# Layer-norm scales and offsets from 16-partition rows spread by matmuls, in place of 1 MB broadcast loads

## The chip, the cores and the metric

The kernel runs on one core of one Trainium2 chip. The metric is device microseconds of that core for one execution, and the median over the runs that were timed. TensorE is written PE, VectorE DVE, ScalarE ACT, GpSimd POOL, SyncE SP. SP issues nearly all plain loads; POOL issues the gathers; all of them are carried by the same 16 DMA engines.

## The reference

For 256 tokens of width 1024 (two blocks of 128 tokens, `tb` 0 and 1), in float32:

```python
for i in range(2):                                   # layers
    mix = mlstm_mixer(x, ...) if i == 0 else mla_mixer(x, ...)
    x = layer_norm(ALPHA * x + mix, ln_g[i, 0], ln_b[i, 0])
    x = layer_norm(ALPHA * x + peer_ffn(x, ...), ln_g[i, 1], ln_b[i, 1])
    x = x + sigmoid(x @ ple_w_gate[i]) * (p[i] @ ple_w_proj[i])
# then second_block: a hybrid attention mixer, a SwiGLU, and a last RMS norm with norm_final_g

def layer_norm(x, g, b):
    y = (x - mean(x)) * rsqrt(var(x) + eps)
    return y * g + b                                 # g, b: 1024 values, the same for all tokens

def peer_ffn(x, w_q, sub_keys, u, v):                # per token: 8 heads, top 16 experts of 16384 each
    act = gelu(u[experts] . x)                       # 128 rows of u a token
    return sum(gates * act * v[experts])             # 128 rows of v a token
```

Every token needs 128 rows of 8 KB (the row of `u` and the row of `v` side by side in `in_uv`) in each of the two layers.

## The kernel before

Tokens lie on the 128 partitions, features along them. The expert rows are the bulk of the traffic: there are four windows `r` = 0 to 3 (layer `r // 2`, token block `r % 2`), and each gathers 128 rows a token as 128 indirect DMAs of 1 MB (128 partitions x 8 KB), L1196, two to a group `k`, 64 groups a window. Eight slots of `gath` hold them. The ring of one group is: POOL waits for `row_free` and issues two gathers; DVE takes the dot product of each landed row with `xt` (L1845); ACT applies Gelu; DVE multiplies with the gate (L1856); ACT scales the `v` half (1024 wide, line 1211); PE adds it, turned, into two held PSUM banks (16 matmuls, L546) and increments `row_free`.

All other work of a window is cut into slots, and `weave` runs so many slots in each group, on each engine between its `head(k)` and its `tail(k)`. The order is the same list of names on PE, ACT and DVE: `sum`, `ple`, `mla`, `attend`, `out`, `pq` (queries and scores of the next layer's experts, the choice of experts on DVE). So the rest of the work moves at the pace of the gathers. Window 0 runs `first_slots`, windows 1 and 2 `next_slots(0)` and `next_slots(1)`, window 3 `last_slots`. What follows the last gather has no gathers beside it.

Weights go through a ring of four slots of 2 MB. `take` on PE appends a load to `loads`, and SP issues the list in order, each as soon as the slot's last use is over. `aux` appends a load of another kind to the same list: the two arrays of a layer norm come this way. `in_lnp` holds them already copied for each of the 128 partitions, so that one `aux` brings `lnp` (128 partitions x 2 x 1024 values). There are six: the first ahead of window 0, then one in `first_slots` (slot 12), one in each `mla_slots` (slot "cq a") and one in each `pq_slots` (slot 6). `ln_apply` on DVE waits for `sem("lnp")`, multiplies by `lnp[:, 0, :]` (L1606) and adds `lnp[:, 1, :]` (L1607). Where the next block of tokens uses the same arrays, `fresh=False`.

PSUM banks are handed out in turn by `open_` (a held bank is passed over), `close` says that a bank is full, and `evac` on ACT copies it out and frees it; `moved` waits for that.

A plain float32 matmul of the code is two MATMUL instructions in the trace (a transpose is one).

Of the kernel before, what the change touches and what calls it, by code (L numbers as in the profile page):

```python
# [14 lines left out]
P = 128  # L15
# [3 lines left out]
KC = D // P  # L19
# [44 lines left out]
X_LAYER = 3  # L64
# [54 lines left out]
def program(nc, a, out, ctx, dbg):  # L119
    def sb(name, shape, dt=F32):  # L120
        return ctx.enter_context(nc.sbuf_tensor(name, shape, dt))
# [13 lines left out]
    yt = sb("y_tok", [P, TB, D])  # L135
    xT = sb("xT", [P, KC, T])
    lnp = sb("lnp", [P, 2, D])
    ident = sb("ident", [P, P])
    identa = sb("identa", [P, P])
    ones = sb("ones", [P, P])  # L140
# [27 lines left out]
    slot_loaded = [sem(f"slot_loaded{i}") for i in range(NW)]  # L168
    x_ready = [sem(f"x_ready{tb}") for tb in range(TB)]
    xn_ready = [sem(f"xn_ready{tb}") for tb in range(TB)]  # L170
    place = {}
    uses = [0] * 8

# [121 lines left out]
    def _(pe):  # L295
# [54 lines left out]

        def aux(dst, src, key, after=None):
            loads.append(dict(kind="aux", dst=dst, src=src, sem=sem(key), after=after))

        def rows(w, c0, n):
            return w[:, c0:c0 + n].rearrange("(k p) n -> p k n", p=P)
# [244 lines left out]
        def mla_slots(tb):  # L600
            transposes("xM", xt, KC, tb, x_ready[tb], X_PLE)
            yield "turn x"
            yield "move x"
            await_T("xM", tb)
            w, rec = take(rows(a["kv_w_down_r"], 0, 512), KC, 512)
            tok(f"ckv_{tb}", xT, w, cols(tb), KV_RANK, KC, slice(0, KV_RANK))
            yield "ckv"
            wq, rq = take(rows(a["b_w_dq"][0], 0, Q_RANK), KC, Q_RANK)
            aux(lnp[:, :, :], a["lnp"][1, 0], "lnp", (x_ready[tb], X_PEER))
            tok(f"cq_{tb}", xT, wq, cols(tb), Q_RANK, KC, ks=range(0, 4))  # L610
            yield "cq a"
            tok(f"cq_{tb}", xT, wq, cols(tb), Q_RANK, KC, ks=range(4, 8))
            last_use(rq, f"cq_{tb}")
            yield "cq b"
            o = open_(f"kr_{tb}")
            for e in range(2):
                ins = feat(o, e * P, w, xT, slice(KV_RANK + e * P, KV_RANK + (e + 1) * P), range(KC), KC, cols(tb))
            close(ins, f"kr_{tb}")
            last_use(rec, f"kr_{tb}")
            yield "kr"  # L620
            yield "rms"
            yield "rms sqrt"
            yield "rms scale"
            pe.wait_ge(sem("c_ready"), tb + 1)
            for nm, c0, n in ((f"ckvT_{tb}", 0, 2), (f"cqT_{tb}", KV_RANK, 3)):
                o = open_(nm)
                for k in range(n):
                    ins = nc.tensor.transpose(o[:, k * P:(k + 1) * P], yt[:, tb, c0 + k * P:c0 + (k + 1) * P],
                                              ident[:, :])
                close(ins, nm)  # L630
            yield "turn c"
            yield "move c"
            moved(pe, f"ckvT_{tb}")
            moved(pe, f"cqT_{tb}")
            wu, rec = take(rows(a["kv_w_up"], 0, 2048), 2, 2048)
            for half in range(2):
                nm = f"kn_{tb}_{half}"
                o = open_(nm)
                for j in range(4):
                    h = half * 4 + j  # L640
                    ins = feat(o, j * P, wu, M["ckvT"], slice(h * 256, h * 256 + 128), range(2), 2, slice(0, P))
                close(ins, nm)
            yield "kn"
            wv = ring[:, rec["slot"], 0:4096].rearrange("p (k h e n) -> p k h e n", k=2, h=H, e=2)
            for half in range(2):
                nm = f"kvv_{tb}_{half}"
                o = open_(nm)
                for k in range(2):
                    ins = mm(o[:, :], M["ckvT"][:, k, :], wv[:, k, half * 4:half * 4 + 4, 1, :], k == 0, k == 1)
                close(ins, nm)  # L650
            last_use(rec, f"kvv_{tb}_1")
            yield "kvv"
            for half in range(2):
                w, rec = take(rows(a["b_w_uq_p"], half * 768, 768), 3, 768)
                nm = f"qn_{tb}_{half}"
                o = open_(nm)
                for j in range(4):
                    ins = feat(o, j * P, w, M["cqT"], slice(j * P, (j + 1) * P), range(3), 3, slice(0, P))
                close(ins, nm)
                nm = f"qr_{tb}_{half}"  # L660
                o = open_(nm)
                for e in range(2):
                    ins = feat(o, e * P, w, M["cqT"], slice((4 + e) * P, (5 + e) * P), range(3), 3, slice(0, P))
                close(ins, nm)
                last_use(rec, nm)
                yield f"q {half}"
            yield "move q"
            yield "rope"
# [66 lines left out]
        def pq_slots(l, tb):  # L735
            transposes(f"xT{l + 1}", xt, KC, tb, x_ready[tb], l * X_LAYER + X_MIX)
            yield "turn x"
            yield "move x"
            await_T(f"xT{l + 1}", tb)
            for i in range(PQ_SLOTS):  # L740
                if i < 8:
                    pq_half(l, tb, i // 2, i % 2)
                if i % 2 == 1 and 0 <= (i - 3) // 2 < 4:
                    scores(l, tb, (i - 3) // 2)
                if i == 6:
                    aux(lnp[:, :, :], a["lnp"][1 if tb else 0, 1], "lnp", (x_ready[tb], X_LAYER + X_MIX))
                yield f"pq {i}"

        def first_slots():
            for i in range(FIRST_SLOTS):  # L750
                if i < 4:
                    pq_half(0, 0, 2 + i // 2, i % 2)
                if i in (1, 3, 5):
                    scores(0, 0, 1 + i // 2)
                if i == 4:
                    transposes("xT1", xt, KC, 1, x_ready[1], X_MIX)
                if i == 6:
                    await_T("xT1", 1)
                if 6 <= i < 14:
                    pq_half(0, 1, (i - 6) // 2, i % 2)  # L760
                if i == 12:
                    aux(lnp[:, :, :], a["lnp"][0, 1], "lnp", (x_ready[1], X_MIX))
                for j, at in enumerate((9, 11, 15, 20)):
                    if i == at:
                        scores(0, 1, j)
                yield f"first {i}"
# [351 lines left out]
    def _(pool):  # L1118
# [19 lines left out]
                          allow_small_or_imprecise_dtypes=True))  # L1138
        step.wait()
        pool.tensor_scalar(identa[:, :], ident[:, :], ALPHA, None, ALU.mult).then_inc(sem("consts"), 1)  # L1140
        pool.wait_ge(sem("gates"), 1)
        for dst, src in ((xt[:, :, :], a["x"].rearrange("(b p) d -> p b d", p=P)), (A["g"][:, :], a["hng"]),
                         (posi, a["pos"]), (invf[:, :], a["invf"])):
# [62 lines left out]
    def _(act):  # L1206
# [21 lines left out]
        def evac_T(name, dst, tb):  # L1228
            for g in range(2):
                evac(f"{name}_{tb}_{g}", dst[:, 4 * g:4 * g + 4, cols(tb)], split(4))  # L1230


        act.wait_ge(sem("c_loaded"), 16)
# [92 lines left out]
        def mla_slots(tb):  # L1326
# [10 lines left out]
            yield "kr"  # L1337
            evac(f"kr_{tb}", M["tk"], split(2))
            yield "rms"
            sqrt(2)  # L1340
            yield "rms sqrt"
            yield "rms scale"
            yield "turn c"
            evac(f"ckvT_{tb}", M["ckvT"], split(2))
# [42 lines left out]
        def pq_slots(l, tb):  # L1387
            n0 = UNIT_BASE[l * TB + tb]
            yield "turn x"
            evac_T(f"xT{l + 1}", xT, tb)  # L1390
            yield "move x"
            for i in range(PQ_SLOTS):
                if i % 2 == 0 and 0 <= (i - 2) // 2 < 4:
                    queries(l, tb, (i - 2) // 2)
                if i % 2 == 0 and 0 <= (i - 4) // 2 < 4:
                    scores(l, tb, (i - 4) // 2)
                m = (i - CHOOSE_FROM - USTEPS) // USTEPS
                if (i - CHOOSE_FROM) % USTEPS == 0 and 0 <= m < UNITS:
                    gate_exp(n0 + m)
                yield f"pq {i}"  # L1400

        def first_slots():
            for i in range(FIRST_SLOTS):
# [5 lines left out]
                    sqrt(1)  # L1409
                if i == 5:  # L1410
                    evac_T("xT1", xT, 1)
                if i in (8, 10, 12, 14):
                    queries(0, 1, (i - 8) // 2)
                for j, at in enumerate((10, 12, 16, 21)):
# [159 lines left out]
    def _(dve):  # L1574
# [2 lines left out]
        nsq = [0]  # L1577
        nln = [0]

        def inverse_sd(n):  # L1580
            nsq[0] += 1
            dve.wait_ge(sem("sd_ready"), nsq[0])
            step(v.reciprocal(rstd[:, 0:n], sdv[:, 0:n]))
# [8 lines left out]
        def ln_apply(tb, src, frees=(), fresh=True, y=None):  # L1592
# [8 lines left out]
                else:  # L1601
                    step(ins)
            if fresh:
                nln[0] += 1
                dve.wait_ge(sem("lnp"), 16 * nln[0])
            step(v.tensor_tensor(y, y, lnp[:, 0, :], ALU.mult))  # L1606
            v.tensor_tensor(xt[:, tb, :], y, lnp[:, 1, :], ALU.add).then_inc(x_ready[tb], 1)  # L1607

# [647 lines left out]
        for tb in range(TB):  # L2256
# [1 line left out]
            dve.wait_ge(x_ready[tb], X_HYBRID + 1)  # L2258
            sum_squares(tb)
            inverse_sd(1)  # L2260
            dve.wait_ge(sem("lnp"), 16 * (nln[0] + 1))
            v.scalar_tensor_tensor(yt[:, tb, :], xt[:, tb, :], rstd[:, 0:1], lnp[:, 0, :], ALU.mult, ALU.mult
                                   ).then_inc(sem("out_ready"), 1)

# [56 lines left out]
```

## Time and profile before

| | |
|---|---|
| median of 3 runs | 2259.17 us (2254.94 to 2259.38) |
| profiled execution: its own time | 2258.05 us |
| its span, first to last instruction | 2256.3 us |
| busy: PE, DVE, ACT, POOL | 1715.9, 1216.9, 907.2, 595.8 us |
| moved by DMA | 777.21 MB, mean 344 GB/s |
| chain that ended last | PE 43%, DMA 31%, DVE 15%, ACT 5%, POOL 3% |

The busy times are sums over the span, and the engines overlap. The chain is followed back from the last instruction, at each step to what released it. The table averages over three parts with different limits: a start of 200 us, the gathers, and an end of some 476 us.

### The profile page before, as it was taken

Reading aid. Unit: us, or ns where it says so; the run is one execution under the profiler, and the core shown is the slowest. Engines: PE = TensorE matmul, PEld = TensorE weight load, DVE = VectorE, ACT = ScalarE, POOL = GpSimd, SP = SyncE. Lnnn points to the kernel's source line nnn. Section 1 sums busy time; section 2 is a strip of 40 time slices with the busy share of each in tenths; the row PEclk is TensorE's granted clock in tenths of the full one; section 3 lists DMA queues with packets and bytes.
Section 4 is the critical chain, followed back from the end, with each engine's and each line's share of the span. In section 5 each row is a group of like instructions: output and inputs, shape, how many; then the busy total and the mean of one; then the engine's idle time right before and its main releaser. Section 6 shows DMA issues by size and latency. Waiting matters only on the chain.

```text
span 2256.3 us, 25092 instructions
## 1 busy us (share of the span) xinstructions
PE 1715.9 (76%) x9720; PEld 1405.1 (62%) x9720; DVE 1216.9 (54%) x3105; ACT 907.2 (40%) x1294; POOL 595.8 (26%) x569
## 2 busy tenths in 40 slices
PE   8998755555767786576778656778877779989998
PEld 6458644445556675455657645468777468868863
DVE  3647687886544559854555896455534255610001
ACT  1113454455544544554455445455654212510000
POOL 1002233444333332333333335543323000000000
PEclk9999876777888797689879867878998888999999
DMA  7639999999999999999999999999999768664350
GB/s 268 244 103 376 415 400 411 400 408 421 386 418 413 416 415 408 405 394 417 413 415 415 397 413 411 409 400 413 410 411 414 274 224 299 235 224 149 112 191 33
DMA packets 183335, 777.21 MB, mean 344 GB/s; under 512 B 11584, under 2 KB 19328, under 8 KB 115888
## 3 DMA queue, kind: packets, MB, share of 16 engines
q0 software_dynamic: 74720, 539.80, 58.4%
q1 hardware_dynamic: 107920, 235.15, 28.3%
q8 instruction: 77, 1.26, 0.2%
q10 hardware_dynamic: 576, 0.66, 0.1%
q14 instruction: 42, 0.34, 0.0%
HBM read 774.52 MB, written 1.05 MB: 344 GB/s over the span
## 4 chain that ended last, share of the span: by engine, by line
PE 43%; DMA 31%; DVE 15%; ACT 5%; POOL 3%; issue 3%; another core or an unknown queue 0%; SPq 0%; DVEq 0%; POOLq 0%; ACTq 0%
PE bank L318 34%; DMA arena<-in_uv,eidx 25%; PE bank L546 9%; DVE arena L1845 5%; DMA ring<-in_peer_w_q 3%; ACT arena L1211 3%; DMA ring<-in_w_in_2r 3%; POOL arena L1196 3%; DVE y_tok L1776 2%; DVE y_tok L1772 1%; ACT L1211 1%; DVE y_tok L1812 1%; DVE y_tok L1813 1%; DVE y_tok L1809 1%; DVE mid_region L1768 0%
## 5 line engine op out<-in xcount | busy, mean ns | idle before, releaser
L546 PE MATMUL bank<-ident,arena 128*128 128x128 f32 x4096 | 663.9, 329 | 421.5 <-ACT arena L1211 421.1
L546 PEld LDWEIGHTS bank<-ident,arena 128*128 128x128 f32 x4096 | 586.3, 171 | 499.4 <-ACT arena L1211 487.9
L1845 DVE CUSTOM_DVE_ANT_0 arena<-arena,x_tok 128x1024 f32<-128x1024 f32 x512 | 621.4, 1224 | 493.7 <-DMA arena<-in_uv,eidx 493.3
L1196 POOL DMA_INDIRECT arena<-in_uv,eidx x512 | 576.3, 1126 | 1139.8 <-PE bank L546 900.8
L1211 ACT ACTIVATE arena<-arena,coef 128x1024 f32<-128x1024 f32 x512 | 559.9, 1141 | 285.2 <-DVE coef L1856 277.0
L318 PE MATMUL bank<-xT,ring 128*128 128x128 f32 (+2 forms) x3104 | 478.0, 317 | 64.7 <-DMA ring<-in_w_in_2r 24.6
L318 PEld LDWEIGHTS bank<-xT,ring 128*128 128x128 f32 (+1 forms) x3104 | 441.5, 202 | 100.2 <-DMA ring<-in_w_in_2r 26.4
L1211 ACT ACTIVATE glu<-dots 128x2 f32<-128x2 f32 x256 | 52.0, 203 | 438.0 <-DVE dots L1845 432.4
L318 PE MATMUL bank<-ring,xT 128*128 128x512 f32 (+3 forms) x384 | 164.2, 583 | 0.0
L1211 ACT ACTIVATE arena<-bank 128x256 f32<-128x256 f32 (+1 forms) x62 | 30.0, 490 | 301.1 <-PE bank L318 295.9
L1211 ACT ACT_TABLE_LOAD x112 | 143.7, 1283 | 2.8 <-PEq L2313 0.8
L318 PEld LDWEIGHTS bank<-ring,xT 128*128 128x128 f32 x384 | 77.2, 207 | 72.1 <-issue 66.0
L318 PE MATMUL bank<-ring,arena 128*128 128x512 f32 x272 | 117.8, 593 | 2.4 <-ACT arena L1211 1.0
L318 PEld LDWEIGHTS bank<-ring,arena 128*128 128x128 f32 x272 | 51.4, 190 | 65.8 <-issue 64.7
L2253 DVE TENSOR_TENSOR arena<-arena,bank 128x256 f32<-128x256 f32 x22 | 9.3, 421 | 150.3 <-PE bank L318 150.3
L1211 ACT ACTIVATE mid_region<-bank 128x512 f32<-128x512 f32 (+7 forms) x108 | 50.4, 493 | 86.8 <-PE bank L318 86.7
L1856 DVE TENSOR_TENSOR coef<-glu,gate 128x2 f32<-128x2 f32 x256 | 41.1, 160 | 64.1 <-ACT glu L1211 60.8
L318 PE MATMUL bank<-ring,mid_region 128*128 128x128 f32 (+1 forms) x240 | 70.3, 440 | 0.5 <-ACT mid_region L1211 0.5
L1625 DVE SCALAR_TENSOR_TENSOR ring<-ring,silu_cT 128x512 f32<-128x512 f32 x84 | 63.2, 752 | 3.0
L318 PE MATMUL bank<-mid_region,ring 128*128 128x128 f32 (+1 forms) x400 | 52.1, 292 | 7.3 <-ACT mid_region L1211 7.3
L318 PEld LDWEIGHTS bank<-mid_region,ring 128*128 128x128 f32 x400 | 51.2, 211 | 7.9 <-ACT mid_region L1211 7.8
L1211 ACT ACTIVATE sdv<-var 128x1 f32<-128x1 f32 (+2 forms) x17 | 3.5, 204 | 129.3 <-DVE var L2048 100.5
(243 smaller groups left out, 1134.0 us busy)
## 6 DMA issues: line engine op xcount, KB each, us to landing
ring<-in_w_in_2r SPq DMA_DIRECT2D x20, 2048.0 KB
ring<-in_peer_w_q SPq DMA_DIRECT2D x16, 2048.0 KB
ring<-in_w_ada SPq DMA_DIRECT2D x12, 2048.0 KB
ring<-in_ple_w_gate SPq DMA_DIRECT2D x8, 2048.0 KB
ring<-in_a_w_in SPq DMA_DIRECT2D x6, 2048.0 KB
ring<-in_w_ffn_gate SPq DMA_DIRECT2D x5, 2048.0 KB
ring<-in_w_ffn_up SPq DMA_DIRECT2D x5, 2048.0 KB
ring<-in_w_ffn_down SPq DMA_DIRECT2D x5, 2048.0 KB
```

The lines of the kernel that those rows point to most:

```text
L318: return nc.tensor.matmul(o, l, r, start=start, stop=stop)
L546: ins = nc.tensor.matmul(bank(f"pe{l}_{tb}_{c // 4}")[:, (c % 4) * P:(c % 4 + 1) * P], gath[:, s, D + c * P:D + (c + 1) * P], ident[:, :], ...
L1196: pool.indirect_dma_start(gath[:, i % SLOTS, :], None, a["uv"], bass.IndirectOffsetOnAxis(ap=eidx[:, tb, i:i + 1], axis=0)).then_inc(sem(f ...
L1211: return nc.scalar.activation(o, i, fn, **kw)
L1625: ins = v.scalar_tensor_tensor(w[:, k, :], w[:, k, :], scT[:, k:k + 1], w[:, k - 1, :], ALU.mult, ALU.add)
L1772: step.go(v.max(vals[:, i, lo:lo + 8], s[:, i, :]))
L1776: step.go(v.max_index(idx[:, i, lo:lo + 8], vals[:, i, lo:lo + 8], s[:, i, :]))
L1809: step(v.tensor_tensor(eq, p12f[:, e, :, :].unsqueeze(3).broadcast_to([P, UH, 16, 16]), iota16[:, :].unsqueeze(1).unsqueeze(1).broadcast_t ...
L1812: step(v.tensor_tensor(eq, eq, i4[:, :, e, :].unsqueeze(2).broadcast_to([P, UH, 16, 16]), ALU.mult))
L1813: step(v.tensor_reduce(i12[:, e, :, :], eq, AX, ALU.add))
L1845: v.tensor_tensor_reduce(out=gath[:, s, 0:D], in0=gath[:, s, 0:D], in1=xt[:, tb, :], scale=1.0, scalar=0.0, op0=ALU.mult, op1=ALU.add, acc ...
L1856: v.tensor_tensor(coef[:, s:s + GRP], glu[:, s:s + GRP], gate[:, tb, k * GRP:(k + 1) * GRP], ALU.mult).then_inc(sem("coef"), 1)
```

## The change

The five norms after the first take their two arrays from `ln_rows`, a small tile. At the start POOL loads, for each of the three pairs (layer, norm) that occur, the 2 x 1024 values once, as 16 rows of 128 values on 16 partitions (partitions 0, 32 and 64 onwards); 8 KB each. Before a norm, `spread(i, e)` on PE (array e of norm i; ten calls) writes the array to all 128 partitions of two PSUM banks: eight matmuls, each with one column of the identity, broadcast to 16 x 128, as the weights and the 16 rows as the moving operand. ACT copies the two banks into `lnp` one slot later, after a wait that the last reader of `lnp` is done. DVE waits for four banks to be moved where it waited for one DMA. Five of the six `aux` loads of `in_lnp` go.

```diff
+        def spread(i, e):                       # PE
+            at = SPREAD_AT[SPREAD[i]]
+            if i == 0 and e == 0:
+                pe.wait_ge(sem("ln_rows"), 16 * len(SPREAD_AT))
+            for half in range(2):
+                nm = f"ln{i}_{e}_{half}"
+                o = open_(nm)
+                for c in range(4):
+                    row = e * KC + half * 4 + c
+                    ins = mm(o[:, c * P:(c + 1) * P], ident[at:at + 16, at + row:at + row + 1].broadcast_to([16, P]),
+                             ln_rows[at:at + 16, :])
+                close(ins, nm)
...
             wq, rq = take(rows(a["b_w_dq"][0], 0, Q_RANK), KC, Q_RANK)
-            aux(lnp[:, :, :], a["lnp"][1, 0], "lnp", (x_ready[tb], X_PEER))
...
             yield "kr"
+            spread(1 + 2 * tb, 0)
             yield "rms"
+            spread(1 + 2 * tb, 1)
             yield "rms sqrt"
...
-                if i == 6:
-                    aux(lnp[:, :, :], a["lnp"][1 if tb else 0, 1], "lnp", (x_ready[tb], X_LAYER + X_MIX))
+                if i in (11, 12):
+                    spread(2 + 2 * tb, i - 11)
...
-                if i == 12:
-                    aux(lnp[:, :, :], a["lnp"][0, 1], "lnp", (x_ready[1], X_MIX))
+                if i in (22, 23):
+                    spread(0, i - 22)
...
+        for (l, i), at in SPREAD_AT.items():    # POOL, behind the constants, ahead of its wait for "gates"
+            pool.dma_start(ln_rows[at:at + 16, :], a["lnp"][l, i, 0].rearrange("e (c n) -> (e c) n", n=P)
+                           ).then_inc(sem("ln_rows"), 16)
...
+        def spread(i, e):                       # ACT
+            for half in range(2):
+                evac(f"ln{i}_{e}_{half}", lnp[:, e, half * 512:half * 512 + 512], whole)
...
             yield "rms"
+            act.wait_ge(x_ready[tb], X_PEER)
+            spread(1 + 2 * tb, 0)
             sqrt(2)
             yield "rms sqrt"
+            spread(1 + 2 * tb, 1)
...
+                if i in (12, 13):
+                    act.wait_ge(x_ready[tb], X_LAYER + X_MIX)
+                    spread(2 + 2 * tb, i - 12)
...
+                if i in (23, 24):
+                    act.wait_ge(x_ready[1], X_MIX)
+                    spread(0, i - 23)
...
+        def norm_loaded():                      # DVE, in ln_apply
+            if nln[0] == 0:
+                dve.wait_ge(sem("lnp"), 16)
+            else:
+                for e in range(2):
+                    for half in range(2):
+                        moved(dve, f"ln{nln[0] - 1}_{e}_{half}")
+            nln[0] += 1
```

## Rows read from the trace of the kernel before

**Rows 1.** The page's 40 slices: busy tenths by engine, then DMA share and GB/s.
```profile
DVE  3647687886544559854555896455534255610001
...
DMA  7639999999999999999999999999999768664350
GB/s 268 244 103 376 415 400 411 400 408 421 386 418 413 416 415 408 405 394 417 413 415 415 397 413 411 409 400 413 410 411 414 274 224 299 235 224 149 112 191 33
```

**Rows 2.** Stretches: from:to, length, busy us (instructions) by engine, PEclk, DMA share, GB/s.
```profile
200.00:1780.00 1580.00, 1092.33 (x6802) 951.61 (x6800) 976.35 (x2498) 795.79 (x1081) 578.50 (x536) 0.81 1.00 406
1780.00:2256.30 476.30, 441.94 (x2157) 336.31 (x2156) 135.19 (x273) 78.06 (x156) 0.55 (x1) 0.94 0.52 187
```

**Rows 3.** DMA queues of the page: packets, MB, share of 16 engines over the span.
```profile
q0 software_dynamic: 74720, 539.80, 58.4%
q1 hardware_dynamic: 107920, 235.15, 28.3%
```

**Rows 4.** Waits over the span: engine line <- releaser: total us, times, longest us.
```profile
POOL arena L1196 <- PE bank L546: 900.8, 222, 21.3
DVE arena L1845 <- DMA arena<-in_uv,eidx: 493.3, 317, 9.5
...
POOL x_tok L1144 <- DVE mid_region L1667: 16.1, 1, 16.1
```

**Rows 5.** DMA issues: the loads into lnp, count and size of each.
```profile
lnp<-in_lnp SPq DMA_DIRECT2D x6, 1024.0 KB
```

**Rows 6.** Timeline of SyncE's queue: start us, us taken, instruction, count.
```profile
221.33 22.27 SPq L1111 DMA_DIRECT2D lnp<-in_lnp  x1
...
598.61 0.66 SPq L1111 DMA_DIRECT2D lnp<-in_lnp  x1
...
823.63 0.58 SPq L1111 DMA_DIRECT2D lnp<-in_lnp  x1
...
998.69 1.22 SPq L1111 DMA_DIRECT2D lnp<-in_lnp  x1
...
1224.36 0.58 SPq L1111 DMA_DIRECT2D lnp<-in_lnp  x1
```

**Rows 7.** Chain of waits, in order: start us, us, what; one gather per load.
```profile
265.40 19.89 DMA arena<-in_uv,eidx
...
606.62 14.46 DMA arena<-in_uv,eidx
...
841.96 18.93 DMA arena<-in_uv,eidx
```

**Rows 8.** Chain of waits, 1195 to 1300 us.
```profile
1223.95 28.80 DMA ring<-in_peer_w_q
...
1252.79 6.44 PE bank L318 x32
...
1280.07 1.14 DVE arena L1845
```

**Rows 9.** Two stretches of DVE choosing experts, columns as in rows 2.
```profile
860.00:920.00 60.00, 33.34 (x186) 29.91 (x184) 57.27 (x186) 29.56 (x37) 20.78 (x20) 0.69 1.01 408
1280.00:1340.00 60.00, 29.62 (x144) 25.64 (x144) 57.51 (x198) 27.14 (x33) 18.50 (x19) 0.66 1.02 413
```

**Rows 10.** VectorE's timeline, 838 to 905 us; in brackets its idle time before.
```profile
860.91 1.23 DVE L1845 CUSTOM_DVE_ANT_0 arena<-arena,x_tok 128x1024 f32<-128x1024 f32 x1 [1.53 <-DMA arena<-in_uv,eidx]
```

**Rows 11.** Stretches of 5 us, columns as in rows 2.
```profile
1265.00:1270.00 5.00, 3.28 (x22) 2.91 (x22) 3.50 (x9) 4.48 (x7) 0.00 (x0) 0.85 0.97 405
1270.00:1275.00 5.00, 3.58 (x24) 3.35 (x23) 4.90 (x24) 3.88 (x6) 3.24 (x3) 0.81 0.69 239
```

**Rows 12.** PE timeline, 860 to 900 us: one score, four matmuls in the code.
```profile
862.69 1.06 PE L318 MATMUL bank<-ring,mid_region 128*128 128x128 f32 x8
```

**Rows 13.** Instruction groups by shape: count, busy us, mean ns, idle before.
```profile
L1211 ACT ACTIVATE y_tok<-bank 128x512 f32<-128x512 f32 x22 | 12.9, 590 | 40.2 <-PE bank L318 36.7 <-PE bank L853 2.9 <-issue 0.5
...
L318 PE MATMUL bank<-mid_region 32*128 32x128 f32 x32 | 5.9, 304 | 0.0
```

**Rows 14.** POOL's timeline, 0 to 60 us.
```profile
24.80 0.56 POOL L1144 DMA_DIRECT2D arena<-in_hng  x1
```

More of the change, by code:

```diff
@@ L137, in program @@
     lnp = sb("lnp", [P, 2, D])
+    ln_rows = sb("ln_rows", [P, P])
     ident = sb("ident", [P, P])
@@ L170, in program @@
     xn_ready = [sem(f"xn_ready{tb}") for tb in range(TB)]
+    SPREAD = ((0, 1), (1, 0), (0, 1), (1, 0), (1, 1))
+    SPREAD_AT = {(0, 1): 0, (1, 0): 32, (1, 1): 64}
     place = {}
@@ L1603, in ln_apply @@
             if fresh:
-                nln[0] += 1
-                dve.wait_ge(sem("lnp"), 16 * nln[0])
+                norm_loaded()
             step(v.tensor_tensor(y, y, lnp[:, 0, :], ALU.mult))
@@ L2260, in _ @@
             inverse_sd(1)
-            dve.wait_ge(sem("lnp"), 16 * (nln[0] + 1))
+            dve.wait_ge(sem("lnp"), 16 * 2)
             v.scalar_tensor_tensor(yt[:, tb, :], xt[:, tb, :], rstd[:, 0:1], lnp[:, 0, :], ALU.mult, ALU.mult
```

## The prediction

> **What bounds the kernel now.** I read the 40 slices first, for where each engine is full. The DMA line is at 9 from the fourth slice to the thirty-first, at some 400 to 420 GB/s in nearly all, and falls off behind it; DVE reaches 9 in two [rows 1]. So I cut the span in parts. From 200 to 1780 us, where the gathers run, the DMA share is 1.00 at 406 GB/s, while PE is busy 1092 of 1580 us, DVE 976 and ACT 796; from 1780 us on the DMA share is 0.52 and PE is busy 442 of 476 us [rows 2]. The reader is to see two limits: bytes in the middle, PE at the end. The change takes no byte and no instruction from the end, so whatever it gives or costs is decided before 1780 us.
>
> The waits agree. DVE waits 317 times, 493.3 us in all, for a gathered row, and POOL 222 times, 900.8 us, for PE to free a slot [rows 4]. Both can be true together because a gather is on its way for long: on the chain of waits, single gathers take 19.89, 14.46 and 18.93 us from the end of their issue to the dot product [rows 7]. The price of one gather alone is far smaller: the gathers' queue held the engines for 58.4% of 2256.3 us, 1317.7 us for 539.8 MB [rows 3], which is 2.56 us for one MB (1.0486 million bytes). Some five to eight gathers' worth of bytes thus stand ahead of each, and it is this queue that sets the pace of the groups, and with it that of all slots woven in.
>
> **What goes.** Six loads of 1024 KB fill `lnp` [rows 5]; five go, issued at 221, 599, 824, 999 and 1224 us [rows 6], all inside the full part. Their rows are 8 KB in one piece on each partition, as the gathered rows are, so I price each at a gather's 2.56 us: 12.8 us for five. The nearest other row is SP's own queue, 28.3% of the span for 235.15 MB [rows 3], 638.5 us, 2.85 us for such a load: 14.2 us, the upper end. Spread over the mean rate of 406 GB/s [rows 2] it is 5.243 / 0.406 = 12.9 us. The lower end is nothing. I take 12.8 us as what leaves the queue.
>
> The Trainium skill (DMA: Bandwidth & Descriptors, Where 436 GB/s comes from) has two ceilings, 435 GB/s where the ports bind and about 358 GB/s where a core's share of the HBM does, and says that the second binds for loads from HBM. By 358 the five loads would be 14.6 us, by 435 12.1 us. This trace holds 406 GB/s over 1580 us of such loads [rows 2], so the 358 does not hold on this core.
>
> **Which of it reaches the end.** Bytes taken away shorten the time only if the DMA engines don't run dry between that load and the next gather somebody waits for; otherwise the pause just becomes longer. I went through the five.
>
> The loads of 599 and 999 us stand in stretches where DVE waits for nearly each row; the gather issued at 606.62 us was waited for [rows 7], and no pause follows before the queue's gain is handed on. Both count in full: 5.12 us. The load of 221 us: the gather ended issuing at 265.40 us took 19.89 us, longer than others, with this load and the next weights ahead of it, and DVE waited [rows 7]. I take 2.3 of 2.56 us.
>
> The load of 824 us: the chain goes over a gather that took 18.93 us [rows 7], but DVE had waited only 1.53 us for it [rows 10], and from there it is nearly full, 57.27 of 60 us [rows 9]. So 1.53 us come at once; what is more only shortens the queue and is worth something when DVE is through. Between 1.53 and 2.56 us I take 1.8.
>
> The load of 1224 us stands behind a weight load on the same queue. The chain goes over that weight load, 28.80 us from 1223.95 us on, then over PE from 1252.79 us on, and DVE is still on it at 1280.07 us [rows 8]. PE's stall held the slots back, and the DMA engines ran nearly dry: share 0.97 and then 0.69 in the 10 us from 1265 us on [rows 11], some 0.05 x 5 + 0.33 x 5 = 1.9 us of pause against the 1.02 of full stretches. Without our load the pause comes to 4.5 us, and nobody gains. Then DVE is full again, 57.51 of 60 us [rows 9]. Bounds nothing and 2.56 us; I take 0.3.
>
> One could hope that the weight load itself lands sooner when the `lnp` load is gone, and with it PE's stall. It is issued first, 0.4 us ahead of ours [rows 6, 8]. The Trainium skill (DMA: Bandwidth & Descriptors, Queues, rings and completion order) says that on each DMA engine one queue's descriptors are taken in ring order; by that the load behind does not slow the one ahead, and this stall stays. If it did slow it, the fifth load would count in full and the sum would be 2.3 us better.
>
> Gain: 5.12 + 2.3 + 1.8 + 0.3 = 9.5 us.
>
> **What comes.** PE: ten calls of eight matmuls, 80 in the code and 160 instructions. The nearest row is a score, 8 instructions in 1.06 us at full clock [rows 12], so 2.1 us a call and 21.2 us in all. The upper bound is the row with few weight rows, 32 x 128: 32 instructions, mean 304 ns each by itself [rows 13], 160 x 0.304 = 48.6 us; its busy time, 5.9 us for 32, gives 29.5 us. The expectation is near the lower value. PE is idle for 488 of the 1580 us [rows 2]. A call delays the rows of its group by 2 to 5 us, and with them the next two gathers; two gathers are 5.1 us of DMA time while 14 to 20 us stand in the queue [rows 7], so the queue doesn't run out. Four of the ten calls come in the choice stretches, where PE is busy 33 and 30 of 60 us [rows 9]. I cost it at nothing. If that cover were gone, it would be the 21 to 49 us themselves.
>
> ACT: twenty copies of a bank, 0.59 us each [rows 13], 11.8 us, in a part where ACT is idle 784 us [rows 2]. In the slot "rms sqrt" two copies come ahead of the square root, 1.2 us later for DVE's normalization, twice; DVE's waits for rows in those stretches cover it. ACT's Gelu is one group ahead of the copies, so DVE's coefficients don't stand behind them. Its new waits on `x_ready` are for steps a dozen slots back. Nothing.
>
> DVE: four bank waits where there was one DMA wait, five norms; all banks were copied many slots before. A passed wait is not in the trace; between nothing and 0.1 us for each of the fifteen more, I take 0.2 us in all. PE's bank rotation moves by two banks a call; the banks come back after six others, long copied. SP loses five issues, one of which held it for 22.27 us [rows 6]; the weights behind it were wanted much later, so nothing. POOL: three more issues, 0.56 us each by a plain one [rows 14], 1.7 us, behind the constants and inside its idle 16.1 us [rows 4]. Their bytes, 24 KB, are 0.06 us.
>
> **Sum.** 9.5 - 0.2 = 9.3 us off the path. The profiled execution took 2258.05 us for a span of 2256.3 us, so 1.75 us lie around it; it would become 2248.75 us. The median of the runs is 1.12 us above this execution; I apply the same difference to it: 2259.17 - 9.3 = 2249.9 us, a change of -0.41%.
>
> **Rivals.** *All five count.* The pause at 1265 us is not independent of our load, the queue hands everything on. Then 12.8 us, 2246.4 us, and with the price of SP's own queue 14.2 us, 2245.0 us. For it: the share is 1.00 over the whole part [rows 2]. Against it: the pause itself [rows 11]. Chance 0.27.
>
> *The queue isn't the limit.* The pace of the groups is that of the loop over PE, ACT and DVE, and faster landing only makes DMA pauses. For it: DVE near full in two stretches [rows 9], POOL's 900.8 us for slots [rows 4]. Against it: 493.3 us of DVE waiting for rows [rows 4]. Only the two loads in stretches without full engines, or less, would count, and the rest of the gain goes: 0 to 4.5 us, 2254.7 to 2259.2 us. Chance 0.14.
>
> *PE's added matmuls decide.* The rows of a group wait for them, the gathers of the next slots are issued later and the queue runs out. If all 21.2 us lay on the path beside the gain of 9.3 us, the time would be 2271.1 us, with 48.6 us 2298.5 us. It is slower than before from the point where 9.3 us of them are on the path, and by over 0.2% from 13.8 us on, 65% of the lower price. For it: PE stands in the ring of each group, and at 1252 us a PE stall did empty the queue [rows 8, 11]. Against it: 488 idle us, and a queue of over 14 us. Chance 0.05.
>
> **How the numbers follow.** The forecast has 0.46: 10.5 us off with the first and third load in full, 8.2 us with 1.53 us for each, and 1.1 us to either side for the step from one execution to the median, so 2247.5 to 2252.5 us. Between it and the second rival, 2252.5 to 2254.7 us, where one more load is lost or some spread calls cost 3 us, lies 0.08. The range from 2244.8 to 2253.8 us takes in the first rival with its dearer price and the forecast, and leaves out the hidden case and the slower one, some 0.2. 0.2% is 4.5 us, about what timing this kernel can tell from no change. Faster by over that: 0.46 + 0.27 + 0.08 = 0.81; within it: 0.14; slower: 0.05.
>
> **What would show it.** The profile after should have five loads fewer, 5.2 MB less, a DMA share still 1.00 and about the same 406 GB/s to the last gather, that gather some 9 us earlier, and the part behind it as long as before (476 us). PE should show 160 instructions more, ACT twenty, and DVE no new wait ahead of L1606. The fifth load's step is right if the pause that follows the last score of window 2 has grown by about 2.5 us, wrong if it hasn't. It would all be wrong if the DMA share fell below 1.00 over the middle with the last gather where it was (the queue was no limit), or if rows came late behind the spread calls.

## The result, and the profile after

The changed kernel has a median of 2247.37 us (2243.91 to 2252.41, 9 runs) beside 2257.91 us for the kernel before (2252.7 to 2262.88, 9 runs): ratio 0.9957, 95% interval 0.9946 to 0.9969, that is 9.7 us less (7.0 to 12.2). The two medians lie 10.5 us apart; the differences in this text go by the ratio, which has the interval. Run again later, it gave 0.9959 (0.9942 to 0.9975), 9.3 us less. The forecast was 9.3 us less.

The page after, first its slices (DVE, DMA share, GB/s), then the DMA queues (packets, MB, share of 16 engines):

```profile
DVE  3648687876544559854455896454534356610001
...
DMA  7639999999999999999999999999999768664350
GB/s 269 246 103 399 415 402 413 403 396 416 401 417 412 417 414 378 400 391 417 413 415 415 391 395 411 410 407 409 413 410 413 279 226 294 248 225 151 113 194 31
```
```profile
q0 software_dynamic: 74816, 539.83, 58.8%
q1 hardware_dynamic: 107200, 229.91, 27.9%
```

SP's queue carries 229.91 MB where it carried 235.15 [rows 3], five loads less; the full part is as full as it was [rows 1]. Cut at its own last gather (from:to, length, busy us with instructions for PE, PEld, DVE, ACT, POOL, then PEclk, DMA share, GB/s):

```profile
200.00:1770.00 1570.00, 1130.34 (x6948) 988.75 (x6949) 975.74 (x2495) 800.86 (x1095) 574.92 (x536) 0.81 1.00 405
1770.00:2242.20 472.20, 436.54 (x2155) 331.85 (x2153) 135.20 (x273) 77.89 (x156) 0.56 (x1) 0.95 0.53 189
```

The gathers' part is 10 us shorter at the same share and rate [rows 2]: fewer bytes, not faster ones. Not all of the 10 us belongs to the change, though. SP issued the weight loads ahead of the first left-out load 4.7 us earlier than before, and the run that keeps all five loads and has the spread calls beside them (below) did it just as early; the profiled execution of the kernel before had lost these microseconds by then. First row before, second after, third the run that keeps the loads:

```profile
201.80 0.99 SPq L1106 DMA_DIRECT2D ring<-in_peer_w_q  x2
197.09 0.99 SPq L1124 DMA_DIRECT2D ring<-in_peer_w_q  x2
197.19 1.00 SPq L1129 DMA_DIRECT2D ring<-in_peer_w_q  x2
```

In the second profile of the changed kernel the last gather was issued at 1746.8 us, against 1742.4 in the first and 1751.6 before. So the size of the effect rests on the runs and their intervals, not on a pair of profiles.

The waits say the same as before [rows 4], with a little less of each:

```profile
POOL arena L1217 <- PE bank L563: 897.0, 227, 17.3
DVE arena L1887 <- DMA arena<-in_uv,eidx: 480.7, 325, 7.0
```

The spreading, as groups by shape (count | busy us, mean ns | idle us before) and two of its ten calls in PE's timeline:

```profile
L322 PE MATMUL bank<-ln_rows,ident 16*128 16x128 f32 x160 | 27.4, 336 | 0.0
L1232 ACT ACTIVATE lnp<-bank 128x512 f32<-128x512 f32 x20 | 10.9, 587 | 7.5 <-PE bank L322 7.5
L1648 DVE TENSOR_TENSOR y_tok<-y_tok,lnp 128x1024 f32<-128x1024 f32 x7 | 8.6, 1225 | 0.2
```
```profile
341.06 3.78 PE L322 MATMUL bank<-ln_rows,ident 16*128 16x128 f32 x16
...
866.77 2.05 PE L322 MATMUL bank<-ln_rows,ident 16*128 16x128 f32 x16
```

The reader is to see three things: 160 instructions as counted, 2.05 us a call at full clock as [rows 12] gave it, and DVE not waiting ahead of its multiplication with `lnp` (0.2 us in seven, and 0.2 us in the kernel before). Four of the ten calls ran at half clock and took 3.78 us, so PE's total is 27.4 us, not 21.2.

This one execution took 2243.91 us, 14.1 us less than the profiled one before, which is more than the 9.7 us of the runs. Some 4 us of the 14.1 arose behind the last gather (472.20 us beside 476.30), in a part that no edit touches; it is told of at the end.

Where the DMA engines paused, and how much, is the part of the prediction that could be wrong. The pause after the scores of window 1, before:

```profile
865.00:870.00 5.00, 4.53 (x40) 4.32 (x40) 4.86 (x14) 4.53 (x8) 1.82 (x2) 1.00 0.98 369
870.00:875.00 5.00, 1.52 (x9) 1.28 (x8) 4.93 (x23) 3.87 (x5) 1.96 (x3) 0.76 0.95 376
```

and after, in window 1 and in window 2:

```profile
850.00:855.00 5.00, 4.86 (x44) 4.66 (x42) 4.41 (x9) 0.70 (x2) 2.92 (x2) 1.00 0.78 283
855.00:860.00 5.00, 3.42 (x20) 3.24 (x21) 3.61 (x8) 4.77 (x6) 0.20 (x1) 0.77 0.82 333
860.00:865.00 5.00, 3.29 (x25) 3.05 (x25) 4.90 (x26) 3.88 (x7) 3.32 (x4) 0.89 0.66 211
```
```profile
1250.00:1255.00 5.00, 4.78 (x43) 4.58 (x41) 4.31 (x9) 0.79 (x2) 2.07 (x2) 1.00 0.98 378
1255.00:1260.00 5.00, 3.50 (x30) 3.32 (x31) 4.09 (x10) 4.77 (x6) 1.09 (x1) 1.00 0.75 306
1260.00:1265.00 5.00, 1.65 (x14) 1.41 (x13) 4.89 (x26) 3.78 (x6) 4.08 (x4) 0.89 0.87 292
```

A pause is counted here as (1.02 - share) x 5 us, summed over the neighbouring rows with a share below 1.00; 1.02 is the share of full stretches. The pause in window 1 was (0.04 + 0.07) x 5 = 0.55 us and is (0.24 + 0.20 + 0.36) x 5 = 4.0 us: it grew by 3.4 us. In window 2 it was 1.9 us [rows 11] and is (0.04 + 0.27 + 0.15) x 5 = 2.3 us. In the second profile of the changed kernel they are 4.0 and 3.4 us.

The weight load ahead of these pauses took as long as before. On the chain of waits it stood with 28.80 us from 1223.95 us on [rows 8]; after, with the `lnp` load behind it gone:

```profile
1214.14 28.64 DMA ring<-in_peer_w_q
```

### The profile page after: what moved, and what is told of

The parts are those of the page before. It is cut to its first block, busy times and chain, and to the rows that moved or that the text cites. A ratio compares the mean times of both kernels' runs of the same rounds, so it can differ in the third digit from the quotient of the medians.

```text
span 2242.2 us, 25444 instructions
## 1 busy us (share of the span) xinstructions
PE 1747.9 (78%) x9880; PEld 1437.5 (64%) x9880; DVE 1217.9 (54%) x3105; ACT 916.7 (41%) x1314; POOL 593.8 (26%) x572
## 3 DMA queue, kind: packets, MB, share of 16 engines
q1 hardware_dynamic: 107200, 229.91, 27.9%
## 4 chain that ended last, share of the span: by engine, by line
PE 46%; DMA 30%; DVE 13%; ACT 6%; POOL 3%; issue 2%; another core or an unknown queue 0%; DVEq 0%; SPq 0%; POOLq 0%; ACTq 0%
PE bank L322 35%; DMA arena<-in_uv,eidx 26%; PE bank L563 10%; DVE arena L1887 4%; ACT arena L1232 3%; DMA ring<-in_peer_w_q 3%; POOL arena L1217 3%; DVE y_tok L1818 1%; ACT L1232 1%; DVE y_tok L1814 1%; DMA ring<-in_w_in_2r 1%; DVE y_tok L1854 1%; DVE y_tok L1855 1%; DVE y_tok L1851 1%; PE bank L399 0%
## 5 line engine op out<-in xcount | busy, mean ns | idle before, releaser
L563 PE MATMUL bank<-ident,arena 128*128 128x128 f32 x4096 | 677.0, 333 | 394.2 <-ACT arena L1232 393.4
L563 PEld LDWEIGHTS bank<-ident,arena 128*128 128x128 f32 x4096 | 598.9, 174 | 471.9 <-ACT arena L1232 459.8
L1887 DVE CUSTOM_DVE_ANT_0 arena<-arena,x_tok 128x1024 f32<-128x1024 f32 x512 | 622.0, 1224 | 481.3 <-DMA arena<-in_uv,eidx 480.7
L322 PE MATMUL bank<-xT,ring 128*128 128x128 f32 (+2 forms) x3104 | 471.4, 314 | 46.5 <-DMA ring<-in_peer_w_q 18.9
L322 PEld LDWEIGHTS bank<-xT,ring 128*128 128x128 f32 (+1 forms) x3104 | 435.5, 199 | 81.1 <-DMA ring<-in_peer_w_q 16.9
```

Source lines behind the costliest of these rows:

```text
L322: return nc.tensor.matmul(o, l, r, start=start, stop=stop)
L563: ins = nc.tensor.matmul(bank(f"pe{l}_{tb}_{c // 4}")[:, (c % 4) * P:(c % 4 + 1) * P], gath[:, s, D + c * P:D + (c + 1) * P], ident[:, :], ...
L1887: v.tensor_tensor_reduce(out=gath[:, s, 0:D], in0=gath[:, s, 0:D], in1=xt[:, tb, :], scale=1.0, scalar=0.0, op0=ALU.mult, op1=ALU.add, acc ...
```

## The experiments

Twelve kernels ran, each beside the kernel before, whose median in these three groups was 2257.0 to 2257.3 us. Ratios are to it. A ratio's interval is some 0.0009 to 0.0015 to either side, 2 to 3.4 us, twice that for the two kernels with four times the spreading, and some 4 us for a difference between two kernels. "The changed kernel" in a difference is its ratio of 0.9957 or 0.9959.

**The parts by themselves.** The changed kernel again:

> The changed kernel once more, beside the three that run with it. Both theories: 9 to 11 us under the kernel before, ratio 0.995 to 0.996 (it measured 0.9957 with an interval of 0.9946 to 0.9969). It is the base for the differences below.

Measured: 2247.98 us, 0.9959.

The kernel before, five loads left out and the semaphore stepped by SP:

```diff
-                sp.dma_start(r["dst"], r["src"]).then_inc(r["sem"], 16)
+                if 1 <= n_aux[0] <= 5:
+                    sp.sem_inc(r["sem"], 16)
+                else:
+                    sp.dma_start(r["dst"], r["src"]).then_inc(r["sem"], 16)
+                n_aux[0] += 1
```

> The kernel before with the five loads left out and nothing in their place: all norms but the first use the first norm's scale and offset, so part of the work is left out. My theory (bytes are worth their time only where no pause of the DMA engines follows, and the spreading costs nothing): the same time as the changed kernel within 1.5 us, 9 to 10 us under before. Rival, all five loads count and the spreading costs some 3 us of it: 12.8 to 14.2 us under before, and 3 us under the changed kernel.

Measured: 2248.95 us, 0.9963 (0.9950 to 0.9976). It is no faster than the changed kernel, so the rival of five full loads less some cost of spreading falls: 12.8 us under before would be 0.9943, outside.

The kernel before with the spread calls run beside its loads (ACT copies each bank onto itself; the cut is against the changed kernel):

```diff
-                evac(f"ln{i}_{e}_{half}", lnp[:, e, half * 512:half * 512 + 512], whole)
+                ps = full(act, f"ln{i}_{e}_{half}")
+                free(f(ps[:, :], ps[:, :], ACT.Copy), f"ln{i}_{e}_{half}")
```

> The kernel before with all five loads kept, and the ten spread calls run beside them: the 160 PE instructions, and twenty bank copies on ACT that write back into the bank, so that nobody uses the result. My theory (all hidden under the queue of gathers): within 1.5 us of before, ratio 0.9993 to 1.0007. Rival, PE's work is on the path: its lower price puts it 21 us above before, ratio 1.009; the rival that the spreading costs 3 us gives 1.0013.

Measured: 2255.44 us, 0.9994 (0.9983 to 1.0005). The work of PE and ACT is free, to within 1.1 us more or 3.8 us less. This run lacks DVE's waits for the banks; the run before it, which has neither them nor the spreading, is no faster than the changed kernel, so they cost nothing that can be seen either.

**How much PE work the gathers cover.** The spread matmuls repeated in place:

```diff
-                for c in range(4):
+                for c in [x for _ in range(4) for x in range(4)]:      # or range(2)
```

> The changed kernel with each spread matmul done four times into the same place (640 PE instructions in place of 160, 27 us of PE become some 100 us, 7 to 8 us more in each of ten calls). My theory: a call delays the next two gathers by 7 to 8 us while 14 us stand in the queue, so most is hidden; 0 to 8 us above the changed kernel. Rival, PE is close to the path: 40 to 80 us above.

Measured: 2303.7 us, 1.0198 (1.0171 to 1.0224), some 54 us above the changed kernel. A clear miss. PE's spread work grew from 27.4 to 120.8 us, more than the expected 7 to 8 us a call, since four calls ran at half clock throughout and took 14.02 us each. The stretches say why it costs time (columns as above), and in the timeline stands one call, with POOL's last issue in it and its next one:

```profile
655.00:660.00 5.00, 5.00 (x46) 4.88 (x45) 3.37 (x11) 2.55 (x4) 1.10 (x1) 1.00 1.02 421
660.00:665.00 5.00, 5.00 (x27) 5.00 (x26) 2.42 (x4) 0.60 (x1) 0.00 (x0) 0.53 1.01 412
...
675.00:680.00 5.00, 5.00 (x26) 5.00 (x24) 1.50 (x4) 0.60 (x1) 0.00 (x0) 0.50 0.94 369
680.00:685.00 5.00, 5.00 (x25) 5.00 (x25) 0.00 (x0) 0.00 (x0) 0.00 (x0) 0.50 0.05 18
685.00:690.00 5.00, 5.00 (x25) 4.78 (x24) 1.42 (x4) 3.99 (x6) 0.38 (x1) 0.50 0.00 0
```
```profile
671.73 14.02 PE L322 MATMUL bank<-ln_rows,ident 16*128 16x128 f32 x64
...
673.52 0.94 POOL L1217 DMA_INDIRECT arena<-in_uv,eidx  x1 [0.30 <-issue]
...
689.62 1.07 POOL L1217 DMA_INDIRECT arena<-in_uv,eidx  x1 [15.16 <-PE bank L563]
```

POOL gets no slot for 15.16 us, and the DMA engines stand still for nearly 10 of them: the cover is the queue, and it is used up. Another call stands just ahead, from 657.1 us on, so two calls in a row have delayed the gathers here.

Twice in place of four times:

> The changed kernel with each spread matmul done twice (320 PE instructions, 27 us of PE become some 55, 2 to 4 us more in each of ten calls). The run with four times gave 56 us for 95 us of PE, so there is a point where the cover ends. Theory A (cover of some 4 us a call, beyond it nearly all counts): 0 to 8 us above the changed kernel. Theory B (a fixed share of all added PE time is on the path, 0.59 as in the run with four times): 16 us above, and then the single spreading must cost 16 us too, which the run with loads and spreads together speaks against.

Measured: 2255.57 us, 0.9985 (0.9971 to 0.9999), 6 us (some 2 to 10) above the changed kernel for 29 us more of PE (56.6 us). A fixed share of 0.59 would be 16 us, outside; a cover of a few us a call, and loss beyond it, fits.

Four times, with ACT's copies two slots later:

```diff
-                if i in (12, 13):
+                if i in (14, 15):
                     act.wait_ge(x_ready[tb], X_LAYER + X_MIX)
-                    spread(2 + 2 * tb, i - 12)
+                    spread(2 + 2 * tb, i - 14)
```

> Four times the spread matmuls as before, and ACT's copies of the spread banks two slots later. ACT stood 90.9 us at these copies waiting for PE in the run with four times. If that wait is the cause (ACT late for its Gelu and its scaling), most of the 56 us go: under 25 us above the changed kernel. If PE itself is the cause (its turning of the rows is late, so slots come free late and the gathers run out), 45 to 60 us above, as without the shift.

Measured: 2295.64 us, 1.0181 (1.0151 to 1.0212), 50 us above the changed kernel. ACT's idle time ahead of the copies went from 90.9 to 15.0 us, the time hardly. ACT's wait was a companion; PE itself is late.

**Which bytes count.** The changed kernel with other loads left out, in the places where the `lnp` loads had stood; as SP steps the semaphore at once, part of the work is wrong:

```diff
-                sp.dma_start(dst, r["src"]).then_inc(slot_loaded[r["slot"]], 16)
+                if r["kc"] == 2 and r["n"] == T + D and seen(r):     # first three in_pT_wp; or: r["n"] == Q_RANK
+                    sp.sem_inc(slot_loaded[r["slot"]], 16)
+                else:
+                    sp.dma_start(dst, r["src"]).then_inc(slot_loaded[r["slot"]], 16)
```

> The changed kernel with the first three loads of in_pT_wp left out (1.31 MB each, 3.93 MB; issued at 231, 823 and 1223 us, right where three of the lnp loads stood, behind the same weight loads, and wanted by nobody before the next window; the products with them are wrong, so part of the work is left out). My theory (bytes ahead of a pause don't count): the first counts, 3.2 us, the other two mostly go into the pauses of 850 to 865 and 1250 to 1265 us, 0 to 1 us each: 3 to 5 us under the changed kernel, some 13 to 15 us under before. Rival (every byte of the full stretch counts): 9.6 us under the changed kernel, 20 us under before.

Measured: 2248.38 us, 0.9964 (0.9949 to 0.9978). 3.93 MB less, and no gain: 1 to 2 us above the changed kernel, some 4 us to either side, where 3 to 5 us under it was expected and full value would be 9.6. Its pauses (windows 1 and 2):

```profile
850.00:855.00 5.00, 5.00 (x48) 5.00 (x47) 4.86 (x9) 0.00 (x0) 2.24 (x2) 1.00 0.42 136
855.00:860.00 5.00, 3.28 (x29) 2.90 (x28) 2.40 (x6) 4.09 (x6) 0.00 (x0) 1.00 0.91 362
860.00:865.00 5.00, 2.73 (x25) 2.49 (x24) 4.89 (x26) 3.78 (x7) 3.86 (x3) 1.00 0.49 178
```
```profile
1250.00:1255.00 5.00, 5.00 (x47) 5.00 (x46) 4.86 (x9) 0.00 (x0) 1.91 (x2) 1.00 0.46 144
1255.00:1260.00 5.00, 3.28 (x29) 2.91 (x28) 2.07 (x6) 4.14 (x6) 0.00 (x0) 1.00 0.89 344
1260.00:1265.00 5.00, 2.69 (x25) 2.45 (x23) 4.90 (x26) 3.77 (x7) 3.86 (x3) 0.99 0.57 177
```

(0.60 + 0.11 + 0.53) x 5 = 6.2 us, and (0.56 + 0.13 + 0.45) x 5 = 5.7 us: together 5.6 us more than the 6.3 of the changed kernel's first profile and 4.5 more than the 7.4 of its second, for 2.62 MB that are worth 6.4 us. Most of the bytes of these two loads has turned into pauses. For the first of the three (window 0) I expected 3.2 us; the whole run leaves little or no room for it, and no single pause there shows where it went. That stays open.

The two loads of `in_b_w_dq` left out:

> The changed kernel with the two loads of in_b_w_dq left out (1.57 MB each, 3.15 MB; issued at 591 and 992 us, where the other two lnp loads stood; the query projection uses what lies in the ring, so part of the work is left out). Both theories: these bytes count in full, 7.7 us under the changed kernel, some 18 us under before. So per MB mine has 2.4 us here and about 1 us in the run without the three others; the rival has 2.4 us in both. If this one gives 3 us or less, my step on the loads of 599 and 999 us falls.

Measured: 2239.43 us, 0.9918 (0.9904 to 0.9933), some 9 us under the changed kernel (5 to 13) for 3.15 MB, where full value is 7.7. Leaving a load out also takes away any wait for it, which would be a rival; but in the changed kernel's trace no engine waits for `in_b_w_dq`, so it is the bytes.

The changed kernel with the `lnp` loads of one kind back:

```diff
+            if i in BY_DMA:          # PE's and ACT's spread; (0, 2, 4) or (1, 3)
+                return
```

The three loads of 221, 824 and 1224 us back:

> The changed kernel with three of the five loads back (those issued at 221, 824 and 1224 us, in the stretches of queries and scores), the other two norms spread by matmuls. My theory (these three were worth 4.4 us, the other two 5.1): 3 to 6 us above the changed kernel, ratio to before 0.997 to 0.9985. Rival one (all equal): 7.7 us above, 0.9992. Rival two (bytes there are never worth anything, as the run without in_pT_wp could be read): no more than 1 us above, 0.996.

Measured: 2253.08 us, 0.9974 (0.9962 to 0.9986). So the two loads of 599 and 999 us, gone alone, give 5.9 us (3.2 to 8.6). If all loads were worth the same it would be 0.9992, outside.

The two loads of 599 and 999 us back:

> The changed kernel with the two other loads back (issued at 599 and 999 us), three norms spread. My theory: 5.1 us above the changed kernel, ratio to before 0.998. Rival one (all equal): the same 5.1. Rival two: these two carry the whole gain of 9.7 us, 1.000.

Measured: 2256.65 us, 0.9992 (0.9984 to 1.0001). So the three others, gone alone, give 1.8 us (0 to 3.6) of their 7.7; on top of the two, 9.5 - 5.9 = 3.6 us, some 4 to either side (9.5 lies between the two measurements of the changed kernel). This is a miss: my 0.998 lies outside the interval, and rival two, 1.000, inside. Read the other way round, the two loads give 9.5 - 1.8 = 7.7 us on top of the three, and 5.9 alone; the intervals of both hold 5.1.

The kernel before with the three loads of `in_pT_wp` left out:

> The kernel before, all lnp loads kept, with the first three loads of in_pT_wp left out (3.93 MB, the products with them are wrong). They gave nothing when the lnp loads were gone. Theory A (the first MB taken from these stretches count until the queue runs dry there, the next don't): 4 to 6 us under before, as the three lnp loads do. Theory B (bytes there never count): within 1.5 us of before. Full value would be 9.6 us.

Measured: 2254.9 us, 0.9985 (0.9975 to 0.9995), 3.4 us of 9.6. Theory A asked for 4 to 6, and B for under 1.5; it lies between, and its interval (1.1 to 5.6 us) touches both. That some of the first MB count in these stretches and further ones don't is the reading that fits best; it isn't shown.

**The two pauses in more profiles.** One profile of a kernel scatters, but there are three in which the loads of 824 and 1224 us stand, and six in which they are gone and neither PE's repeats nor `in_pT_wp` were touched. Their pauses behind the scores of windows 1 and 2, counted as above from rows of 5 us:

| profile | loads of 824 and 1224 us | window 1, us | window 2, us |
|---|---|---|---|
| before | there | 0.55 | 1.9 |
| before, spread calls beside the loads | there | 0.95 | 1.35 |
| changed, three loads back | there | 1.45 | 2.2 |
| changed kernel, first and second profile | gone | 4.0 and 4.0 | 2.3 and 3.4 |
| before, five loads left out | gone | 2.4 | 3.5 |
| changed, the two loads of 599 and 999 us back | gone | 3.05 | 2.3 |
| changed, `in_b_w_dq` left out | gone | 3.45 | 2.8 |
| changed, scales of the low-rank norms too (below) | gone | 3.7 | 2.75 |
| mean | there; gone | 1.0; 3.4 | 1.8; 2.8 |

The pause of window 1 grew by some 2.4 us, nearly the whole 2.56 us of its load, and that of window 2 by 1.0 us. It is the missing load that does it and not the spreading: the kernel before with five loads left out has no spreading, and the one with the spread calls beside its loads has all of it.

**A version with still fewer bytes.** Scales of the two low-rank norms from five rows, DVE reading the bank:

```diff
-            act.dma_start(M["cg"], a["kvg"]).then_inc(sem("mla_par"), 16)
-            act.dma_start(yt[:, tb, 640:1024], a["qng"]).then_inc(sem("mla_par"), 16)
...
+            for nm, r0, n in (("cg", 0, 2), ("qg", 2, 3)):
+                o = open_(f"{nm}_{tb}")
+                for c in range(n):
+                    row = 96 + r0 + c
+                    ins = mm(o[:, c * P:(c + 1) * P], ident[96:101, row:row + 1].broadcast_to([5, P]), ln_rows[96:101, :])
+                close(ins, f"{nm}_{tb}")
```

> The changed kernel with the two rows of the low-rank norms (kv_norm_g, b_q_norm_g) treated the same way: five rows on partitions 96 to 100 loaded once, ten more matmuls of five rows in all, DVE reads the scales from the bank, and the four loads of 128 and 192 KB that ACT issued at 630 and 1030 us go, 0.66 MB of the stretch whose bytes count. My theory: 1.6 us under the changed kernel, ratio to before 0.995; too small to be told apart by itself. Rival (the small loads were also waited for, 10 to 14 us from issue to landing): 3 us or more under it. If the added PE work or the wait for the bank were on DVE's path it would be above it.

Measured: 2246.32 us, 0.9949 (0.9936 to 0.9962), the lowest ratio of a kernel that computes everything. It is below the kernel before, beyond its interval, and below the changed one by 2 us, which its interval can't tell from nothing.

## Why the prediction was right, point by point

The total was forecast at 9.3 us and came to 9.7 and 9.3. That it fits so closely is partly luck: the intervals are 2.6 us and more to either side, and below the sum two terms look wrong in opposite directions (the loads of 824 and 1224 us).

*The limit.* Right: bytes until the last gather, and none of the bytes' rate changed. Leaving the five loads out by themselves gives 8.3 us (5.4 to 11.3), the whole effect within the intervals.

*The cost of spreading at nothing.* Right in time, and shown by running it beside the loads. The 0.2 us that I put down for DVE's waits had no row behind it, and no run can show so little; its idle time there is the same as before. The size of PE's work was short, 27.4 for 21.2 us, since four calls fell into half clock. The reason given for the cover was right in kind and too generous in size: I wrote that 14 us of gathers stand in the queue, as if all were cover. Doubled work already costs some 6 us. PE's 488 idle us were no measure of it: what counts is how long the rows of one group may be late before the gathers run out, a few us. The slower rival's mechanism is real: with calls four times as large, some 54 us came of 93 us more of PE.

*The two loads of 599 and 999 us, 5.12 us.* Right within the intervals: 5.9 us measured alone (3.2 to 8.6), and the other loads of the same place had full value.

*The three others, 2.3 + 1.8 + 0.3 = 4.4 us.* Taken alone they give 1.8 us (0 to 3.6), so the term is too large there; on top of the two it is 3.6 us, which can't be told from 4.4. The rule was right, that bytes ahead of a pause only lengthen it. I applied it fully to the load of 1224 us alone, because there the pause stood in the trace. The load of 824 us was of the same kind: behind the same weight load, ahead of the same PE stall and the same DVE stretch; before the change its pause was only 0.55 us, and I took that for the absence of one. With the load gone the pause is larger by some 2.4 of the load's 2.56 us, so hardly anything is left of my 1.8. For the load of 1224 us I asked for 2.5 us more of pause; it is 1.0 in the mean (0.4 and 1.5 us in the two profiles of the changed kernel). By the sign that I gave this step isn't confirmed, and up to 1.5 us of that load may reach the end, where I had 0.3. No run has the load of 1224 us by itself, nor that of 221 us: the run without `in_pT_wp` says that bytes near the latter give little or nothing more, but not where they went.

*The weight load ahead lands no sooner.* Right: 28.80 us before, 28.64 us after.

*The first rival, all five count,* is out by the run with the loads left out. *The queue isn't the limit* is out as a total, 0 to 4.5 us against the measured 9.7 (7.0 to 12.2); the three loads by themselves give 1.8 us of their 7.7, which is its mechanism. *PE decides* is out at single size, and true at four times the size.

Two ends of the forecast's band were added up loosely. The first and third load in full give 10.3 us off and not 10.5; with 1.53 us for each it is 8.3 and not 8.2, and so with 1.1 us for the step to the median the band is 2247.7 to 2252.0 us and not 2247.5 to 2252.5. The measured 2247.37 us lies just below it, because the kernel before came out at 2257.91 us over nine runs where I had 2259.17 over three; the change of 9.7 us lies between 8.3 and 10.3.

## What to carry to other kernels

A stretch whose DMA share is 1.00 is not yet one in which every byte counts: look which engine the chain of waits runs on behind the load; where it leaves the DMA engines before the next awaited transfer, the byte saved can become a pause, even if the trace shows next to none yet (0.55 us here, 4.0 after). Moving broadcast work from DMA to PE in such a stretch is free only up to the slack of the ring of buffers, which is a few us at a time here and far less than PE's idle sum of 488 us. A single profile places gains badly: two pauses of like cause took 4.0 and 2.3 us in one execution of the changed kernel, 4.0 and 3.4 in the next, and 2.4 and 3.5 in the run with the loads left out.

## What was not expected of the hardware

PE at half clock while fully busy. In the run with four times the spreading PE is busy 5.00 us in each of the 5 us rows from 655 to 665 us, and the granted clock falls from 1.00 to 0.53 between them, while the 16-row matmuls of a spread call run. From 675 to 690 us, with PE again busy in full, it is 0.50, that is 1.2 GHz; a call of 64 instructions took 14.02 us there. It is back at 0.89 in the row from 690 us on, where 128-row matmuls have run since 685.68 us. The Trainium skill (TensorE: Matmul & The Clock Gate, What's actually happening) says that activity releases the throttle. Here being busy with these matmuls did not, and why stays open.

The last part of the span has more than one length, whatever the kernel. PE waits there for a chain of DVE, and behind it ran 24 matmuls in 8.49 us in the profile before and in 5.73 us in the one after (chain of waits of each; start us, us, what):

```profile
1907.84 8.49 PE bank L318 x24
```
```profile
1897.19 5.73 PE bank L322 x24
```

The granted clock in the 5 us windows from 1905 and from 1910 us was 0.68 and 0.64 before, and 1.00 in those from 1895 and 1900 us after. From the load issue ahead of it to the one behind, 15.51 us passed before and 12.34 after; 12.34 in the second profile of the changed kernel too, but 15.53 in the one with five loads left out. It isn't the edit: over the fourteen profiles the 24 matmuls took 5.73 us in four, one of which keeps all loads, and 6.17 to 8.74 us in the others, 8.51 in the one that also spreads the scales of the low-rank norms. Of the 14.1 us between the two profiled executions, 3.2 are this.
